# S5 products in four tiles of the array, grouped at chunks 0 and 14; most of the S5 tables' arithmetic on ACT

## What is computed

```python
u = rmsnorm(h, g_pre)
p = u @ w_in                       # (256, 4096) @ (4096, 12296), float32
...                                # p is split into 13 parts
# S5: 64 groups of 16 features, 64 complex states each
lam_bar = jnp.exp(lam * dt)
b_bar = ((lam_bar - 1.0) / lam)[..., None] * b_c
bu = jnp.einsum('gph,blgh->blgp', b_bar, uf.astype(jnp.complex64))
states = _linear_scan(jnp.broadcast_to(lam_bar, bu.shape), bu)
y = jnp.einsum('ghp,blgp->blgh', c_c, states).real
y = y + d_skip * uf
y = jax.nn.gelu(y)
y = y * jax.nn.sigmoid(y @ w_glu + b_glu)
...                                # two attentions, RG-LRU, all gated by silu
mixed = jnp.concatenate([o_fox, o_sb, o_ssm, o_lru], axis=-1) @ w_out
return h + rmsnorm(mixed, g_post)
```

## Time and profile before

| | |
|---|---|
| median of 3 runs | 1628.36 us (1624.19 to 1628.96) |
| the profiled execution | 1625.05 us, of it 1623.3 us from first to last instruction |
| granted TensorE clock, mean | 0.996 |
| busy share PE, DVE, ACT, POOL | 97%, 62%, 51%, 13% |
| the S5 stage (eight query and key blocks) | 207.1 us to about 648.5 us |
| the source blocks 1 to 3 | about 66.5 us to 199.7 us |

### The profile page before, as it was taken

The page is one execution under the profiler, slowest core; times in us unless marked ns, Lnnn a source line. Parts: engine busy times, 40 slices in busy tenths (PEclk is TensorE's granted clock), DMA queues, the critical chain, the costliest instruction groups (busy, mean ns, idle before and its releaser), DMA issues.

```text
span 1623.3 us, 24918 instructions
## 1 busy us (share of the span) xinstructions
PE 1582.6 (97%) x8238; PEld 1329.9 (82%) x8238; DVE 1003.5 (62%) x1238; ACT 820.3 (51%) x1083; POOL 210.4 (13%) x282
## 2 busy tenths in 40 slices
PE   8999999999999999999999999999999999999995
PEld 7888878777877787888888888888888888888884
DVE  6654477897798779545555554556557544444444
ACT  6644344445444444666655554466667444444442
POOL 0000053245225522000001110100000000000000
PEclk9999999999999999999999999999999999999998
DMA  8566645555555555656555555556556876666674
GB/s 299 161 186 178 192 137 172 176 147 158 171 172 154 158 170 168 198 165 208 162 188 171 165 155 169 159 177 181 155 173 189 276 207 193 194 194 193 193 237 152
DMA packets 85574, 294.38 MB, mean 181 GB/s; under 512 B 9504, under 2 KB 11808, under 8 KB 85536
## 3 DMA queue, kind: packets, MB, share of 16 engines
q1 hardware_dynamic: 77184, 276.86, 56.5%
q10 hardware_dynamic: 8352, 17.03, 3.1%
HBM read 289.66 MB, written 4.19 MB: 181 GB/s over the span
## 4 chain that ended last, share of the span: by engine, by line
PE 58%; issue 28%; POOL 6%; DVE 5%; ACT 3%; POOLq 0%; DVEq 0%; ACTq 0%
PE main L252 14%; PE main L273 11%; PE main L275 11%; PE main L274 10%; PE main L254 7%; PE side L384 2%; POOL scr L1202 1%; ACT w_hi L471 1%; POOL scr L1205 1%; DVE vals L974 1%; DVE vals L980 1%; DVE vals L981 1%; POOL scr L1209 1%; POOL scr L1224 1%; POOL scr L1207 1%
## 5 line engine op out<-in xcount | busy, mean ns | idle before, releaser
L741 DVE TENSOR_TENSOR w_lo<-w_raw,w_hi 128x1024 fp32r<-128x1024 f32 x512 | 643.1, 1261 | 527.6 <-ACT w_hi L471 524.6
L252 PE MATMUL main<-acts,w_hi 128*128 128x512 f32 x2560 | 912.3, 400 | 3.2 <-DVE acts L874 1.9
L471 ACT ACTIVATE w_hi<-w_raw 128x1024 fp32r<-128x1024 f32 x512 | 535.1, 1057 | 602.1 <-PE main L254 336.9
L254 PE MATMUL main<-acts,w_lo 128*128 128x256 f32 x2560 | 716.4, 280 | 0.0
L252 PEld LDWEIGHTS main<-acts,w_hi 128*128 128x128 f32 x2560 | 480.3, 188 | 129.6 <-issue 10.7
L254 PEld LDWEIGHTS main<-acts,w_lo 128*128 128x128 f32 x2560 | 483.2, 189 | 0.5
L273 PE MATMUL main<-w_hi,acts 128*128 128x512 f32 x768 | 300.6, 391 | 0.0
L275 PE MATMUL main<-w_hi,acts 128*128 128x512 f32 x768 | 298.9, 389 | 0.0
L274 PE MATMUL main<-w_lo,acts 128*128 128x512 f32 x768 | 298.8, 389 | 0.0
L275 PEld LDWEIGHTS main<-w_hi,acts 128*128 128x128 f32 x768 | 144.2, 188 | 30.3
L273 PEld LDWEIGHTS main<-w_hi,acts 128*128 128x128 f32 x768 | 144.2, 188 | 29.9 <-DVE w_lo L741 0.2
(11 more groups left out here) (233 smaller groups left out, 982.9 us busy)
## 6 DMA issues: line engine op xcount, KB each, us to landing
w_raw<-in_wall SPq DMA_DIRECT2D x512, 512.0 KB, 3.6
br<-in_x SPq DMA_DIRECT2D x16, 256.0 KB, 8.1
scr<-in_bt ACTq DMA_DIRECT2D x8, 512.0 KB, 3.4
scr<-in_wglu ACTq DMA_DIRECT2D x8, 512.0 KB, 4.1
out<-br SPq DMA_DIRECT2D x8, 512.0 KB, 3.1
br<-in_gpost ACTq DMA_DIRECT2D x8, 256.0 KB, 5.3
vals<-in_x ACTq DMA_DIRECT2D x8, 256.0 KB, 5.1
scr<-in_x ACTq DMA_DIRECT2D x8, 256.0 KB, 4.3
```

What stands on the lines that cost most here:

```text
L252: pe.matmul(main[:, j, :], w_hi[:, s, at:at + P], acts[:, k, :], start=(k == 0), stop=False)
L254: mm = pe.matmul(main[:, j, T:2 * T], w_lo[:, s, at:at + P], acts[:, k, 0:T], start=False, stop=(k == NK - 1))
L471: act.activation(w_hi[:, c % RING, :], w_raw[:, c % RING, :], ACT.Copy).then_inc(hi_ready, 1)
L741: dve.tensor_tensor(w_lo[:, c % RING, :], w_raw[:, c % RING, :], w_hi[:, c % RING, :].bitcast(F32), ALU.subtract).then_inc(lo_ready, 1)
```

## The change

- **PE, inputs.** `s5_inputs` runs once a block, in front of chunk 0, for all four parts: for r, for j, a product of 32 rows by 128 columns of weights (`s5_bt[32j:32j+32, r, :]`) with the 32 matching rows of `s5_u`. The four parts lie in four row groups of the array and write four PSUM banks.
- **PE, outputs.** `s5_outputs` runs once a block, in front of chunk C_AT = 14: for r, for j, the products with 32 weight columns, to four column groups and one bank. `s5_h` has four buffers in place of two.
- **DVE** starts part 0 at chunk 0 in place of 2 and ends at chunk 11 in place of 13; it waits no more for the output products. It takes the next block's parameters and inputs (`take_s5`) at chunk 11, and makes y at chunk 14.
- **Tables.** ACT computes angle and rounding (`turns`: three operations) and the cosine (an `Identity` with scale -1 and bias 1, behind the square). POOL keeps one subtraction for each part and the six output factor operations. ACT's `tables(0)` comes before the first `high` of the block, at chunk 0; the others come at chunks 1, 4 and 7, `turns` at chunks 14 (for the next block), 0, 3 and 6.
- **Transfers.** The input weights come as four transfers of 32 partitions by 1 KB, issued by ACT at chunk 5 of the block before (the first before source block 1), in place of one of 512 KB at chunk 0.
- **Order.** The forget gate's 32 products (line 321) move from behind source block 3 to behind source block 0, with ACT's copy and DVE's sum of them. The last of the eight blocks is written out behind a loop of seven on ACT and DVE. One `Gelu` over all eight tiles takes the place of eight.

```diff
-        s5_h = [vflat[:, 1536:2048], vflat[:, 2048:2560]]
+        s5_h = [vflat[:, 1536:2048], vflat[:, 2048:2560], scr[:, 256:768], scr[:, 4400:4912]]
...
-        s5_bt = scr[:, 0:1024].rearrange("p (j r s) -> p j r s", j=SJ, r=2)
+        s5_bt = scr[:, 0:256].rearrange("p (r s) -> p r s", r=2)
...
+        C_AT = CH - 2
+        TURN_AT, TRIG_AT = (CH - 2, 0, 3, 6), (0, 1, 4, 7)
...
             with pe.Fori(0, B_V - B_QK) as i:
-                def s5_inputs(j):
-                    if j == 0:
-                        pe.wait_ge(su_ready, i + 1)
-                        pe.wait_ge(bt_in, i * 16 + 16)
-                    if j >= 2:
-                        pe.wait_ge(s5_done, i * SJ + j - 1)
+                def s5_inputs():
+
+                    pe.wait_ge(side_free, i + 1)
+                    pe.wait_ge(su_ready, i + 1)
+                    pe.wait_ge(bt_in, i * 64 + 64)
                     for r in range(2):
-                        mm = pe.matmul(side[:, j % 2, r * T:(r + 1) * T], s5_bt[:, j, r, :], s5_u[:, :],
-                                       start=True, stop=True)
-                    mm.then_inc(s5_bmm, 1)
...
+                        for j in range(SJ):
+                            rows = slice(32 * j, 32 * j + 32)
+                            mm = pe.matmul(side[:, j, r * T:(r + 1) * T], s5_bt[rows, r, :],
+                                           s5_u[rows, :], start=True, stop=True)
+                            if r == 1:
+                                mm.then_inc(s5_bmm, 1)
+
+                def s5_outputs():
+
+                    pe.wait_ge(s5_cprime, i + 1)
+                    pe.wait_ge(s5_done, i * SJ + SJ)
+                    for r in range(2):
+                        for j in range(SJ):
+                            mm = pe.matmul(side[32 * j:32 * j + 32, 0, 0:T], s5_cp[:, j, r, :],
+                                           s5_h[j][:, r * T:(r + 1) * T], start=(r == 0), stop=(r == 1))
+                    mm.then_inc(s5_cmm, 1)
+
+                for c in range(CH):
+                    if c == 0:
+                        s5_inputs()
+                    if c == C_AT:
+                        s5_outputs()
                     chunk_fm(i + B_QK, i + B_QK, c)
...
+            def turns(f, j):
+
+                act.wait_ge(p5_ready, f + 1)
+                turn = s5_now[:, j:j + 1]
+                act.activation(s5_a, steps_t, ACT.Copy, scale=turn).then_inc(s5_ang, 1)
+                act.activation(s5_k, steps_t, ACT.Copy, scale=turn, bias=ROUND).then_inc(s5_ang, 1)
+                act.wait_ge(s5_ang, f * (3 * SJ) + 3 * j + 2)
+                act.activation(s5_k, s5_k, ACT.Copy, bias=-ROUND).then_inc(s5_ang, 1)
...
+                def tables(j):
+
+                    act.wait_ge(s5_frac, i * SJ + j + 1)
+                    if j >= 2:
+                        act.wait_ge(s5_done, i * SJ + j - 1)
+                    act.activation(s5_sin[j % 2][:, 0:T], s5_f, ACT.Sin, scale=-TWO_PI).then_inc(s5_trig, 1)
+                    act.activation(s5_sin[j % 2][:, T:2 * T], s5_f, ACT.Sin, scale=TWO_PI).then_inc(s5_trig, 1)
+                    act.activation(s5_q, s5_f, ACT.Sin, scale=TWO_PI / 2).then_inc(s5_trig, 1)
+                    act.wait_ge(s5_trig, i * 4 * SJ + 4 * j + 3)
+                    act.activation(s5_q, s5_q, ACT.Square, scale=math.sqrt(2.0)).then_inc(s5_trig, 1)
+                    act.wait_ge(s5_trig, i * 4 * SJ + 4 * j + 4)
+                    act.activation(s5_cos[j % 2], s5_q, ACT.Identity, scale=-1.0, bias=1.0).then_inc(s5_cosd, 1)
+
+                for c in range(CH):
+                    if c == TRIG_AT[0]:
+                        tables(0)
                     high(i + B_QK, c + LEAD)
...
+                    if c in TRIG_AT[1:]:
+                        tables(TRIG_AT.index(c))
+                    if c in TURN_AT[1:]:
+                        turns(i, TURN_AT.index(c))
+                    if c == TURN_AT[0] and not isinstance(i, int):
+                        turns(i + 1, 0)
+                    if c == 5 and not isinstance(i, int):
+                        act.wait_ge(s5_bmm, i * SJ + SJ)
+                        load_inputs(i + 1)
...
-            for f in range(FT):
-                act.activation(br[:, SSM0 + f, :], br[:, SSM0 + f, :], ACT.Gelu_apprx_tanh).then_inc(gelu_done, 1)
+            act.activation(br[:, SSM0:SSM0 + FT, :], br[:, SSM0:SSM0 + FT, :],
+                           ACT.Gelu_apprx_tanh).then_inc(gelu_done, 1)
...
+                    if c == 3 * SJ - 1 and not isinstance(i, int):
+                        dve.wait_ge(s5_cprime, i + 1)
+                        dve.wait_ge(s5_done, i * SJ + SJ)
+                        take_s5(i + 1)
+                    if c == C_AT:
+                        dve.wait_ge(s5_cmm, i + 1)
+                        y = br[:, SSM0 + i, :]
+                        dve.scalar_tensor_tensor(y, y, pars[:, bass.ds(i + PC["ssm_d"][0], 1)], side[:, 0, 0:T],
+                                                 ALU.mult, ALU.add).then_inc(side_free, 1)
...
+                    g = i * SJ + j
+                    pool.wait_ge(s5_ang, g * 3 + 3)
+                    if j:
+                        pool.wait_ge(s5_trig, g * 4)
+                    pool.tensor_tensor(s5_f, s5_k, s5_a, ALU.subtract).then_inc(s5_frac, 1)
```

More of the change, by code:

```diff
@@ L538, in _, with load_inputs @@
                     copy_cross(0, 0)
+            act.wait_ge(fl_mm, 1)
+            act.activation(fl_cross[0:2 * FT, :], side[0:2 * FT, 3, T:2 * T], ACT.Copy).then_inc(fl_act, 1)
+            def load_inputs(f):
+                for j in range(SJ):
+                    rows = slice(32 * j, 32 * j + 32)
+                    act.dma_start(s5_bt[rows, :, :], bt[bass.ds(f, 1), rows, j * 2 * P:(j + 1) * 2 * P]
+                                  .rearrange("f p (r s) -> (f p) r s", r=2)).then_inc(bt_in, 16)
+            act.wait_ge(wf_lo, 1)
+            load_inputs(0)
             with act.Fori(1, B_QK - B_SRC) as i:
@@ L928, in _, with take_s5 @@
                     source_tiles(0)
+            dve.wait_ge(fl_act, 1)
+            dve.tensor_tensor(fl_rows[0:2 * FT, :], side[0:2 * FT, 3, 0:T], fl_cross[0:2 * FT, :],
+                              ALU.add).then_inc(side_free, 1)
+            def take_s5(f):
+                dve.tensor_scalar(s5_now, s5par[:, f, :], 1.0, None, ALU.mult).then_inc(p5_ready, 1)
+                dve.tensor_scalar(s5_u, br[:, SSM0 + f, :], 1.0, None, ALU.mult).then_inc(su_ready, 1)
+            dve.wait_ge(pd, n_pd)
+            dve.wait_ge(br_ready, 1)
+            take_s5(0)
             with dve.Fori(1, B_QK - B_SRC) as i:
@@ L947, in _ @@
                     low(i + B_QK, c + LEAD)
[L948 to L953, removed]
+                    if c // 3 < SJ:
+                        j, part = c // 3, c % 3
                         g, done = i * SJ + j, i * (7 * SJ) + 7 * j
-                        sin, cos, hs = s5_sin[j % 2], s5_cos[j % 2], s5_h[j % 2]
-                        bu = side[:, j % 2, :]
+                        sin, cos, hs = s5_sin[j % 2], s5_cos[j % 2], s5_h[j]
+                        bu = side[:, j, :]
                         if part == 0:
@@ L994, in _ @@
                                                  rs_banks, ALU.mult, ALU.mult).then_inc(br_ready, 1)
-            dve.wait_ge(gelu_done, FT)
+            with dve.Fori(0, B_V - B_QK - 1) as i:
+                s5_block(i)
+            s5_block(B_V - B_QK - 1)
+            dve.wait_ge(gelu_done, 1)
             dve.wait_ge(fl_mm, 2)
@@ L1057, in _ @@
             dve.wait_ge(fl_act, 4)
-            dve.wait_ge(fl_dve, 3)
+            dve.wait_ge(fl_dve, 2)
             dve.wait_ge(glu_applied, 1)
@@ new lines, in fraction, with output_factors @@
+                    g = i * SJ + j
[3 more added lines that the diff above has]
+                    pool.tensor_tensor(s5_f, s5_k, s5_a, ALU.subtract).then_inc(s5_frac, 1)
+                def output_factors():
+                    now = lambda n: s5_now[:, n * SJ:(n + 1) * SJ].unsqueeze(2).to_broadcast([P, SJ, 2 * HG])
+                    pool.wait_ge(ct_in, i * 16 + 16)
+                    pool.wait_ge(s5_bmm, i * SJ + SJ)
+                    c_re, c_im = s5_ct[:, :, 0, :], s5_ct[:, :, 1, :]
+                    for n, (part, factor) in enumerate(((c_re, 2), (c_im, 4), (c_re, 4), (c_im, 3))):
+                        pool.tensor_tensor(s5_c[n], part, now(factor), ALU.mult).then_inc(s5_cq, 1)
+                    pool.wait_ge(s5_cq, i * 5 + 4)
+                    pool.tensor_tensor(s5_cp[:, :, 0, :], s5_c[0], s5_c[1], ALU.add).then_inc(s5_cq, 1)
+                    pool.wait_ge(s5_cq, i * 5 + 5)
+                    pool.tensor_tensor(s5_cp[:, :, 1, :], s5_c[2], s5_c[3], ALU.add).then_inc(s5_cprime, 1)
@@ L1229, in _ @@
                 for j in range(SJ):
-                    cosine(j)
-                    if j + 1 < SJ:
-                        fraction(j + 1)
+                    fraction(j)
```

(1 more changed line is left out.)

94 lines of the change are left out of this document (17 added, 77 removed).

## The result

The changed kernel takes **1566.97 us** (median of 4 runs, 1563.88 to 1567.4) against 1627.3 (4 runs, 1624.19 to 1628.96): ratio 0.9627, 95% interval 0.9607 to 0.9647. The profiled execution took 1563.88 us, span 1562.0, against 1625.05 before: 61.2 us less. Of all executions of all versions one, of the version with the output group at chunk 15, was slow (2079 us, mean granted clock 0.688) and enters no comparison.

The account below looks back on a forecast made before the run. The prediction took PE, busy for 97% of the span, as the bound: 5.4 us a block, 43.5 us for eight, plus 1.2 us for Gelu, total 44.7 us off 1628.4, gives 1584 us; range 1568 to 1610.

Parts of the forecast that it names:

- The products: PE's 16 small S5 products a block: half overlap between tiles, 3.84 us in place of 6.83; chance 0.40.
- the changes of shape: PE switching between 128x128 and narrow products: four round trips a block become two, 1.5 us becomes 0.75.
- full overlap: Rival: PE's small products run four tiles at a time, both groups 2.85 us a block, 1576 us; chance 0.26.
- The wait at chunk 7: PE's input products waiting there for DVE's `s5_done`: goes, since `side` holds all four parts; worth 1.7 us a block.
- The tables: Sine and cosine arithmetic moved from POOL to ACT: no direct gain on PE's path, ACT at about 33 of 50 us.
- POOL's remainder: POOL's work left in an S5 block after the tables move: about 5.5 of 21.3 us.
- DVE's schedule: Whether DVE finishes the last part before PE's output group at chunk 14: yes, 2.3 us early.
- T0: The end of a block on PE, from which the forecast counts DVE's and PE's times in the next block.
- The room: Time between DVE's last part (T0 + 39.6) and PE reaching chunk 14 (T0 + 41.9): 2.3 us.
- that rival: Late tables: `Identity` on ACT needs its own table loads, the last part slips past chunk 14, 1606 us; chance 0.11.
- the drain at each tile change: Rival: each step to the next tile within PE's groups costs time, at 0.35 us each 1647 us; chance 0.05.
- Gelu: One operation in place of eight: PE's wait for DVE at chunk 4 of the first value block vanishes, 1.2 us.

Follow-up runs that it names:

- The loop order run: The changed kernel with the two loops of each product group exchanged (for j, for r in place of for r, for j): 1568.19 us, ratio to before 0.963.
- The chunk 8 run: The kernel before with the group of chunk 7 (inputs of part 2, outputs of part 0) in front of chunk 8: 1630.4 us, ratio 1.0017.
- the 32-row run: The kernel before with each part's input products on only its 32 rows, at their old places: 1627.57 us, ratio 0.9998.
- the tables alone: The kernel before with angle, rounding and cosine on ACT, products neither tiled nor moved: 1619.83 us, ratio 0.9951.

## Why the prediction was right and wrong

**The products: wrong, and this is the step that failed.** "Only the second half of one product and the first of the next can run together" gave 3.84 us for both groups. Measured, less the 0.75 for the changes of shape, they take 1.7: full overlap, 2.1 us less in each of the eight blocks, 17 us, which is the whole distance from 1584 to 1567. The loop order run shows the premise wrong, since tiles don't wait for each other's place in the list. Full overlap was in the text with chance 0.26, but priced at 2.85 us and 1576 us, 9 too many. That size, and with it the range, failed mainly on one term: I took the pace of weight loads, 0.11 us, from loads that all go to one row group and made it a floor for loads to four. It is none (sixteen in 0.74). With 2.45 in place of 3.6 for groups and changes of shape the full case gives 1576 - 9 = 1567, the measured time. That the range came within 1 us of it is luck: its lower end counted on a quicker pace of the main pairs, and they kept 0.353 us. A bound read from a row holds only for what the row has in common with the new case, and this one lacked the very thing that the change brings.

The Trainium skill ("TensorE: Matmul & The Clock Gate", section on packing small matmuls) would have given an estimated 1571 by its figure of 3.07 times, nearer than mine. Here eight products take about 0.9 us by the start distances less the change of shape, in place of 3.4: 3.8 times. Its statement that matmuls start in program order does not agree with the starts shown above.

**Changes of shape: right.** 0.25 us of "issue" ahead of the 32-row group, as ahead of the others.

**The wait at chunk 7: right in size, wrong in kind.** It was worth the 1.7 us a block forecast. I took it as what two buffers in `side` cost, and as gone with them. The chunk 8 run and the 32-row run show that it was DVE's lateness in the first ten chunks; the tables alone remove most of it.

**The tables: wrong.** "Nobody on PE's path gains from this directly" was a poor reading of the row it used. The change needs it: without it DVE's 48.1 busy us are more than the 47.7 that PE now needs, and 23 of the 60 us are lost (13 with the outputs at chunk 15). I had the slowdown of `low` in hand and did not add it up over all of DVE's operations against a shorter block. POOL's remainder was sized too small as well: 8.1 us a block in place of about 5.5, since its operations took longer than in the rows used (the subtraction 0.99 us on average in place of 0.74), so POOL's busy time fell by 104 us and not by 125.

**DVE's schedule: right.** First `low` at T0 + 4.8 us (forecast 4.9), last part at T0 + 40.1 (39.6). The room was 0.8 and not 2.3: PE came 1.0 us sooner, by the overlap, and the last part 0.5 later. One table load, `Identity` without one: right; that rival fell. So did the drain at each tile change, by 1.27 and 1.18 us a group.

**Gelu:** the wait of 1.2 us in the first value block went, as forecast; no run changes the Gelu or the forget gate's place alone. Sum: 60.8 for eight blocks + 1.2 - 0.3 for the wait in the first block = 61.7, measured 61.2.

## What to carry over

Small fp32 products that use 32 rows or 32 columns of the array should stand together, each in a tile of its own; their order within the group is free, and a group of eight costs about two. When PE's part of a block gets shorter, add up the other engines' busy time against the new length first: here DVE would have been the bound, and it was made to fit by taking traffic from POOL, although neither was on PE's list. When a wait is moved and turns up again at the next place, the late engine is the bound, not the place.

## What the hardware showed that was not expected

- PE's granted clock fell to 1.2 GHz though PE was busy without a gap, behind seven of eight groups of 3.7 us of matmuls in one row group of 32 rows; the same number of products on 128 rows (3.4 us), on four row groups (0.9), or on 128 rows and one column group of 32 columns (3.4), left it at 2.4 GHz. It also fell behind all seven waits of 1.93 to 3.19 us in front of the output group, behind one of three waits of 1.93 us in front of 128-row products, and behind none of up to 1.8 us.
- Matmuls in different tiles did not start in the order of the list: parts 2 and 3 began at 299.99 us, ahead of three halves of part 0, which stand before them.
- Weight loads to four row groups overlap: 16 in 0.74 us, against 4 in 0.52 for one.
- The same pairs of main products run at 0.347 or 0.353 us apart, in stretches; over a block that is 0.7 us. What decides stays open.
- POOL's operations cost DVE some 0.3 us of extra busy time for each us that POOL works (43.2 to 48.1 us a block for 8.1 to 25.6); how that goes on between or beyond these two points is not shown.
